# Other homes in SBUF for the weight ring and the attention outputs of a two-layer attention kernel

## What is computed

```
for l in range(2):                      # first block
    h = rmsnorm(x, attn_norm_g[l])
    qa, ka, va, ga, cq, ckv, kr, gb = split(h @ w_in[l])
    ya = swa_attention(qa, ka, va, swa_sinks[l]) * silu(ga)      # 16 heads of 64, window 128
    yb = mla_attention(cq, ckv, kr, ..., w_q_b[l], w_kv_b[l]) * silu(gb)   # 8 heads of 128
    x = x + concat([ya, yb]) @ w_out[l]
x = rmsnorm(x, final_norm_g)
hs = concat([meta_tokens, x])           # second block, one layer
q, k, v, g_attn, u, g_pool, m_attn, m_pool = split(rmsnorm(hs) @ w_in_2)
y_attn = (stick_breaking_attention(q, k, v) * silu(g_attn)) @ w_attn_up_2
y_pool = (pool(u) @ pool_w_2 * pool_scale_2 * silu(g_pool)) @ w_pool_up_2
hs = hs + (sigmoid(m_attn) * y_attn + sigmoid(m_pool) * y_pool) @ w_out_2
return rmsnorm(hs)[:, N_META:]
```

## Time and profile before

| | |
|---|---|
| median of three runs | 2918.37 us |
| the profiled execution, its own time | 2917.28 us |
| its span, first to last instruction | 2915.6 us |
| mean granted TensorE clock | 0.981 |
| TensorE busy | 2836.3 us, 97% of the span |
| TensorE weight loads | 2323.9 us, 80% |
| VectorE, ScalarE, GpSimd busy | 1314.8, 995.5, 1091.3 us |
| DMA, mean | 99 GB/s |

### The profile page before, as it was taken

One profiled execution on the slowest core, in us unless ns is written; L12 is line 12 of the kernel. 1 busy time (PEld: TensorE's weight loads), 2 busy tenths in 40 slices (PEclk: granted clock), 3 DMA queues, 4 the chain that ended last, 5 costly groups with the idle time before them and its releaser, 6 DMA issues.

```text
span 2915.6 us, 33754 instructions
## 1 busy us (share of the span) xinstructions
PE 2836.3 (97%) x13316; PEld 2323.9 (80%) x13316; DVE 1314.8 (45%) x1816; ACT 995.5 (34%) x1557; POOL 1091.3 (37%) x536
## 2 busy tenths in 40 slices
PE   7999999999999999999999999999999999999997
PEld 5888887778888888777887778788878888888886
DVE  6646555741455565474336444544334222222323
ACT  5233434522323334352333332333223233222321
POOL 3443332234444333213443333333444444444442
PEclk9999998999999999899999999999999999999998
DMA  5332231134433222213443222222222333336333
GB/s 160 101 110 71 67 116 42 45 106 137 139 99 120 70 73 73 92 38 85 137 145 87 73 73 73 73 73 77 82 91 94 114 122 115 109 113 206 115 130 108
DMA packets 307613, 288.11 MB, mean 99 GB/s; under 512 B 33152, under 2 KB 256000, under 8 KB 306944
## 3 DMA queue, kind: packets, MB, share of 16 engines
q1 hardware_dynamic: 300656, 263.93, 30.3%
q10 hardware_dynamic: 6800, 22.02, 2.0%
HBM read 259.66 MB, written 26.21 MB: 98 GB/s over the span
## 4 chain that ended last, share of the span: by engine, by line
PE 80%; DVE 12%; ACT 5%; issue 1%; POOL 1%; DMA 1%; DVEq 0%; SPq 0%; ACTq 0%
PE bank L828 23%; PE bank L830 22%; PE bank L829 22%; PE work L828 2%; DVE probs L1564 2%; PE work L830 1%; PE work L829 1%; PE o_bank L828 1%; PE work L1049 1%; PE o_bank L829 1%; PE o_bank L830 1%; DVE pt L1572 1%; DVE mixed L1136 1%; ACT w_hi L678 1%; DVE mixed L1135 1%
## 5 line engine op out<-in xcount | busy, mean ns | idle before, releaser
L819 POOL TENSOR_TENSOR w_lo<-w_raw,w_hi 128x1024 fp32r<-128x1024 f32 (+3 forms) x468 | 1002.5, 2144 | 1518.0 <-ACT w_hi L678 1518.0
L828 PE MATMUL bank<-act_in,w_hi 128*128 128x512 f32 x2664 | 1057.3, 397 | 27.2 <-DVEq L1223 13.5
L830 PE MATMUL bank<-act_in,w_lo 128*128 128x512 f32 x2664 | 1043.1, 392 | 0.0
L829 PE MATMUL bank<-act_in,w_hi 128*128 128x512 f32 x2664 | 1042.2, 391 | 0.0
L678 ACT ACTIVATE w_hi<-w_raw 128x1024 fp32r<-128x1024 f32 (+3 forms) x468 | 437.9, 937 | 1065.6 <-PE bank L830 632.0
L828 PEld LDWEIGHTS bank<-act_in,w_hi 128*128 128x128 f32 x2664 | 502.5, 189 | 135.8 <-POOL w_lo L819 19.0
L830 PEld LDWEIGHTS bank<-act_in,w_lo 128*128 128x128 f32 x2664 | 502.1, 188 | 108.0
L829 PEld LDWEIGHTS bank<-act_in,w_hi 128*128 128x128 f32 x2664 | 503.1, 189 | 99.5 <-issue 1.4
L828 PE MATMUL bank<-mixed,w_hi 128*128 128x512 f32 x768 | 300.1, 391 | 0.0
L830 PE MATMUL bank<-mixed,w_lo 128*128 128x512 f32 x768 | 299.3, 390 | 0.0
L829 PE MATMUL bank<-mixed,w_hi 128*128 128x512 f32 x768 | 299.3, 390 | 0.0
(11 more groups left out here) (247 smaller groups left out, 2915.9 us busy)
## 6 DMA issues: line engine op xcount, KB each, us to landing
w_raw<-in_w_in SPq DMA_DIRECT2D x512, 128.0 KB, 2.4
w_raw<-in_w_in SPq DMA_DIRECT2D x224, 256.0 KB, 2.9
w_raw<-in_w_out SPq DMA_DIRECT2D x64, 512.0 KB, 3.6
w_raw<-in_w_in SPq DMA_DIRECT2D x32, 512.0 KB, 3.7
w_raw<-in_w_out SPq DMA_DIRECT2D x64, 256.0 KB, 4.7
probs<-in_xT SPq DMA_DIRECT2D x32, 256.0 KB, 5.0
x_scr<-buf ACTq DMA_DIRECT2D x32, 256.0 KB, 3.0
probs<-x_scr SPq DMA_DIRECT2D x32, 256.0 KB, 5.0
```

What stands on the lines that cost most here:

```text
L819: nc.gpsimd.tensor_tensor(lo, raw, hi, ALU.subtract).then_inc(lo_ready, 1)
L828: pe.matmul(dst, lhs[0], rhs[0], start=start, stop=False, skip_group_check=skip)
L829: pe.matmul(dst, lhs[0], rhs[1], start=False, stop=False, skip_group_check=skip)
L830: return pe.matmul(dst, lhs[1], rhs[0], start=False, stop=stop, skip_group_check=skip)
```

## The change

Homes alone are changed. `w_hi` and `w_lo`, one tensor each with three slots, become lists of three tensors each. Six small tensors (`r_meta`, `meta_acc`, `fold`, `sinks`, `sinks8`, `stat`) move from behind the large ones to between the slots, and take the room that sets the slots 64 bytes apart modulo 512. `mixed` and what follows it start 256 bytes later, behind an unused tensor. Instructions, their order on each engine, shapes, steps and semaphores are the same in both kernels: 20201 instructions, each equal to its partner but for the addresses.

```diff
         act_in = sb("act_in", [P, KT, 2, T], F32R)
+        sb("mixed_shift", [P, 64])
         mixed_at = nc.sbuf_base
         mixed = sb("mixed", [P, KT, 2, T], F32R)
...
-        w_hi = sb("w_hi", [P, RING, 2, T], F32R)
-        w_lo = sb("w_lo", [P, RING, 2, T], F32R)
+        w_hi, w_lo = [], []
+        w_hi.append(sb("w_hi0", [P, 2, T], F32R))
+        r_meta = sb("r_meta", [P, META])
+        w_hi.append(sb("w_hi1", [P, 2, T], F32R))
+        meta_acc = sb("meta_acc", [P, META])
+        w_hi.append(sb("w_hi2", [P, 2, T], F32R))
+        sinks = sb("sinks", [P, 2, 16])
+        sinks8 = sb("sinks8", [P, 2, 16])
+        stat = sb("stat", [P, 8, NB])
+        w_lo.append(sb("w_lo0", [P, 2, T], F32R))
+        fold = sb("fold", [2 * META, META])
+        w_lo.append(sb("w_lo1", [P, 2, T], F32R))
+        sb("w_lo2_shift", [P, 16])
+        w_lo.append(sb("w_lo2", [P, 2, T], F32R))
...
-        r_meta = sb("r_meta", [P, META])
-        meta_acc = sb("meta_acc", [P, META])
-        fold = sb("fold", [2 * META, META])
...
-        sinks = sb("sinks", [P, 2, 16])
-        sinks8 = sb("sinks8", [P, 2, 16])
-        stat = sb("stat", [P, 8, NB])
...
-                src, dst = w_raw[:, c % RAW, 0:nk, 0:w], w_hi[:, c % RING, 0:nk, 0:w]
+                src, dst = w_raw[:, c % RAW, 0:nk, 0:w], w_hi[c % RING][:, 0:nk, 0:w]
...
-                hi, lo = w_hi[:, c % RING], w_lo[:, c % RING]
+                hi, lo = w_hi[c % RING], w_lo[c % RING]
```

More of the change, by code:

```diff
@@ L809, in _ @@
                 raw = w_raw[:, c % RAW, 0:nk, 0:w]
-                hi = w_hi[:, c % RING, 0:nk, 0:w].bitcast(F32)
-                lo = w_lo[:, c % RING, 0:nk, 0:w]
+                hi = w_hi[c % RING][:, 0:nk, 0:w].bitcast(F32)
+                lo = w_lo[c % RING][:, 0:nk, 0:w]
                 if chunks[c][1] == "swa":
@@ L911, in meta_product @@
                     x = meta_in[:, kt, :, :].rearrange("p s t -> p (s t)")
-                    pe.matmul(work[0][0:2 * META, 0:256], x, w_hi[:, c % RING, kk, cols],
+                    pe.matmul(work[0][0:2 * META, 0:256], x, w_hi[c % RING][:, kk, cols],
                               start=first and kk == 0, stop=False, skip_group_check=True)
-                    ins = pe.matmul(work[0][0:META, 0:256], x[:, 0:META], w_lo[:, c % RING, kk, cols],
+                    ins = pe.matmul(work[0][0:META, 0:256], x[:, 0:META], w_lo[c % RING][:, kk, cols],
                                     start=False, stop=last and kk == 1, skip_group_check=True)
@@ L1096, in _ @@
                             cols = slice(128 * m, 128 * m + 128)
-                            ins = three(work[1 + m][:, :], (w_hi[:, c % RING, kk, cols], w_lo[:, c % RING, kk, cols]),
+                            ins = three(work[1 + m][:, :], (w_hi[c % RING][:, kk, cols], w_lo[c % RING][:, kk, cols]),
                                         (pooled[:, kk, 0], pooled[:, kk, 1]), kk == 0, kk == 1)
```

## The result

| | before | after |
|---|---|---|
| median of three runs | 2918.37 us | 2945.82 us (2943.78 to 2947.28) |
| ratio | | 1.0094 [1.0071, 1.0117] |
| the profiled execution, its own time | 2917.28 us | 2945.82 us |
| its span | 2915.6 us | 2944.2 us |
| mean granted TensorE clock | 0.981 | 0.982 |

The account below looks back on a forecast made before the run. TensorE's large 512-column matmuls were taken to bound the kernel. Every part added 0 to the profiled 2917.3 us; the median after was put at 2918.0 us, range 2909 to 2924 us.

Parts of the forecast that it names:

- What bounds the kernel: TensorE, busy 97% of the span, mostly with 10296 large 512-column matmuls, 226.2 ns each in two 200 us stretches.
- Distance costs 0 ns: TensorE's large matmuls: distances 256 and 384 seen at no cost, 320 not seen; 0 ns taken for all.
- meta products: Two small TensorE matmuls, weights at 0, moving operand at 128: distance 384, 115 ns each, read as no cost.
- Small matmuls as a test: Small matmuls in the kernel before, with weights away from the moving operand's home, were taken to show distance costs nothing.
- distances on both sides: Argument against a cost at distance 320 in the large matmuls: 256 and 384 cost nothing.
- upper bound of 14 ns: Worst case for a large matmul at the unseen distance: 240 ns after the meta products less 226.
- slot 1 pays for its distance of 320: Rival: 2664 large matmuls with `act_in` slow by 14 ns each, 37 us, giving 2955 us; chance 4%.
- a clash of the two reads at equal homes: Rival: large matmuls leaving distance 0 gain 13 ns each, 124 us, giving 2794 us; 3%, smaller gains 8%.
- surplus of 13 ns: Time of each large matmul not explained by its 512 columns at 2.4 GHz; worth 134 us over 10296.
- ScalarE, GpSimd, VectorE, DMA at nothing: Moved homes were taken to cost 0 on the engines beside TensorE and in transfers.
- The forecast is wrong if the pace moves by more than 0.5 ns: Test on the large matmuls: 10296 x 0.56 ns = 5.8 us, what the measurement can tell from no change.
- every third chunk runs at over 0.23 us: Expected sign if slot 1 pays: every third chunk over 0.23 us from start to start, the others not.

Follow-up runs that it names:

- first run: The kernel before, with everything behind `act_in` 256 bytes later, the ring in one home at distance 256 to `act_in`: 2916.97 us against 2918.29, ratio 0.9993.
- tenth: The kernel before, its large products using only 32 of each 128 weight columns, ring at distance 0: 2947.28 us against 2918.68, one run.
- eleventh: The kernel before, its large products using only 32 of each 128 weight columns, ring at distance 64: 2952.79 us against 2918.68, one run.
- mended kernel: The changed kernel with its small tensors reordered so each slot lies a multiple of 256 bytes from `act_in` and `mixed`: 2918.03 us against 2917.26, ratio 1.0001.
- ninth experiment: The kernel before, with ring slots 4, 8 and 16 bytes off as views of one tensor: 2942.87 us against 2918.68, one run.
- fourth run: The kernel before, with `r_meta` moved ahead of `act_in`, so all homes from there on shift 64 bytes at distance 0: 2919.32 us, ratio 1.0004.
- third: The kernel before, with `r_meta` moved ahead of the ring, so all slots are at distance 64: 2963.31 us, ratio 1.0152.
- eighth: The run of the mended kernel: 2918.03 us against 2917.26, ratio 1.0001.
- second: The changed kernel, with the 256 bytes taken from before `mixed` and put before the ring, `mixed` and `w_raw` back at 128: 2946.02 us, ratio 1.0100.
- seventh run: The kernel before, with all `w_hi` slots at distance 0 and all `w_lo` slots at distance 64: 2946.23 us, ratio 1.0103.
- run 9: The kernel before, with ring slots at distances 4, 8 and 16 bytes: 2942.87 us against 2918.68, one run.
- run 5: The kernel before, with the ring's slots 32, 96 and 160 bytes beyond their old home: 2963.19 us against 2917.26, one run.
- run 3: The kernel before, with `r_meta` moved ahead of the ring, all slots at distance 64: 2963.31 us, ratio 1.0152.
- run 6: The kernel before, with the ring's slots 64, 192 and 224 bytes beyond their old home: 2958.55 us against 2917.26, one run.

## Why the prediction was wrong

- **What bounds the kernel:** right. The large matmuls' pace set the time before and after, and the stretches of the earlier trace rows showed the loss in one look.
- **Distance costs 0 ns:** this step failed. It was right for 256, which the first run showed over whole stretches. It was wrong for 320, the distance not seen, and for 384, which I called seen "at no cost and no gain". The 384 rested on the meta products of the earlier trace rows: 256 columns streamed, 32 and 16 columns of weights. The tenth and eleventh runs show that large matmuls with weights of 32 columns take the same in the mean at distances 0 and 64, so that row could not speak for weights of 128.
- **Small matmuls as a test:** this is the error beneath. All rows of small matmuls I used were at distance 256 or 0, which are the same, or had narrow weights; and matmuls of 256 columns with full weights later turned out to go another way with the distance than those of 512 (last section), so they were no stand-in either. "I take 0 ns for all of them" joined three distances of which only one had been seen under the conditions of the ring. That "distances on both sides" cost nothing bore on 320 only if the cost were smooth between them.
- **Its upper bound of 14 ns** for a matmul held: the largest loss measured is 7.6 ns, at distance 96. That it held is luck in part: the row behind it shows the slow matmuls after the meta products, at distance 0. By my count these take 224 to 236 ns, some 231 in the mean of the first nine, which is near the pace of distances off 0; that the two have one cause is not shown.
- **The rival "slot 1 pays for its distance of 320"** was the right mechanism, with a chance of 4% and two mistakes in size. Slot 2 pays as well, with `act_in` and with `mixed`, and so does slot 1 with `mixed`. The price is 6.7 ns (slot 1) and 5.8 ns (slot 2) in 3504 and 3336 matmuls, 43 us at the steady pace, of which 34.8 us are measured as new. It had 14 ns in 2664, 37 us.
- **The rival "a clash of the two reads at equal homes"** was wrong in sign. Equal homes are the best of all places tried, and the surplus of 13 ns over 213.3 is still there in them. By what the Trainium skill says of the ports ("SBUF — State Buffer", Who interferes with whom) homes would be indifferent; with weights of 128 columns the runs show otherwise, 226.7 against up to 234.3 ns.
- **ScalarE, GpSimd, VectorE, DMA at nothing:** right. GpSimd's full chunk has a mean of 2455 ns, line 1242 (1235 before) 690 ns, and the mended kernel, in which all of these are moved, takes 1.0001 of the time. It holds for the moves of this change, all multiples of 64 bytes. The ninth experiment, with 4 and 8 bytes, shows GpSimd's chunk 16% shorter, so this says nothing of smaller offsets.
- **"The forecast is wrong if the pace moves by more than 0.5 ns":** it moved by 4.2 ns in the stretches named. The line "every third chunk runs at over 0.23 us" was two of three.

**What is settled:** the loss comes from the distance of the weights to the moving operand modulo 256 bytes. It doesn't come from the home itself (fourth run), from slots that differ (third, eighth), or from the shift of `mixed` (first, second). Undoing the distances undoes it (eighth).

**What is open:** why. The state at 226.67 ns looks like one in which load and stream keep step, and which any offset of a word or more, a narrower load or a small matmul before breaks; that is an argument, not shown. The order 228, 229, 236 of the seventh run, the uneven table below and GpSimd's gain in the ninth have no explanation here. No version ran faster than the kernel before by more than the noise; one with the ring at distance 0 and `w_raw` or VectorE's tensors a few bytes off was not tried.

## What to carry to other kernels

In this kernel, full-width matmuls of 512 float32 columns load new weights each time. Where yours do the same, put the weights and the streamed operand at the same place modulo 256 bytes; a small tensor of 64 bytes allocated between them cost 1.5% here. To know whether such a thing matters, count the starts in a stretch where TensorE is never idle, and take the evidence only from rows with the same columns on both operands. When a sum takes zero for something unseen, its price times the number of instructions is the range, even if one distance on each side seems free.

## What the runs showed of the hardware

The pace of a 512-column matmul with 128 columns of weights, at the clock's upper level, by the distance of the weights modulo 256 bytes (my count in the timelines):

```
distance   ns        from
0          226.7     before, runs 1, 4 and 8, slot 0 of after
4          232.5     run 9
8          230.6     run 9
16         233.2     run 9
32         233.3     run 5
64         233.4     run 3, slot 1 of after
96         234.3     run 5
128        232.5     slot 2 of after
160        233.3     run 5
192        229.4     run 6 with act_in; 231.7 with mixed
224        233.3     run 6
```

- At the lower clock the distance costs nothing: the large matmuls start 423 to 427 ns apart at every distance of the table (139 intervals at 0, 64 at 64, 1 to 12 at each other), which is 512 columns at 1.2 GHz.
- 256-column matmuls with `act_in` as the weights go another way: 119.5 ns at distance 0 (before), 117.1 ns at 192 (third run) and 117.0 at 224 (fifth), but 122.6 at 252 (ninth). Here are their groups, of the kernel before and of the third run; the modelled durations show the same 2 to 3 ns:

```profile
L829 PE MATMUL bank<-w_lo,act_in 128*128 128x256 f32 x64 | 18.1, 282 | 0.0
```

```profile
L829 PE MATMUL bank<-w_lo,act_in 128*128 128x256 f32 x64 | 17.8, 279 | 0.0
```

- Fewer columns of weights make a matmul of 512 columns slower, by 3.3 ns at 64 columns and 5.0 ns at 32, although the load is 55 and 80 ns shorter.
- GpSimd's 1024-element subtraction takes 2091 and 2031 ns with the ring 4 and 8 bytes off its old home, against 2489 and 2424 in the same slots before; 16 bytes and all the larger moves leave it within some 2% (ninth experiment and the others).
